# Skip weights loaded as a row, and the first half of the output projection's first block placed between the steps of the last sample stream

## The chip, the cores and the metric

The kernel runs on one core of a Trainium2 chip. TensorE (PE) multiplies, VectorE (DVE), ScalarE (ACT) and GpSimd (POOL) do the elementwise work, and SyncE (SP) issues nearly all transfers. The metric is the time of one execution on the device in microseconds, as the median of several runs.

## The reference

One inference step of a hybrid encoder of two layers over 512 prompt tokens and 8 samples of 16 tokens each (640 columns in all). Layer 0 mixes tokens by sparse attention, layer 1 by a Mamba-2 scan; an MLP follows each mixer. The two places that matter here are the end of the attention (its output projection) and the skip weights of the scan:

```python
def dsa_mixer(h, past_k, past_v, past_ik, w_in, w_o, rel_bias):
    ...
    out = jnp.swapaxes(out, 0, 1).reshape(b, t, N_HEADS * HEAD_DIM)
    return out @ w_o, k, v, ki

def ssd_mixer(h, conv_state, ssm_state, w_in, conv_w, conv_b, dt_bias, a_log, d_skip, norm_w, w_out):
    ...
    dt = jax.nn.softplus(dt_raw.astype(jnp.float32) + dt_bias.astype(jnp.float32))
    ...
    y, final = ssd_scan(xs, dt, A, Bm, Cm, init, blk)
    y = y + xs * d_skip.astype(jnp.float32).reshape(SSM_GROUPS, HEADS_PER_GROUP)[..., None]
```

`w_o` is 1024 x 1024. `d_skip` (the input `ssm_d`) has one number for each of 32 heads.

## The kernel before

Activations lie transposed in SBUF: 1024 features as 8 chunks of 128 partitions, 640 tokens as columns. A product of 32-bit precision is made of three: each operand is split into a high part (ACT copies it to a rounded type: `WH`, `b1H`) and a low part (DVE subtracts: `WL`, `b1L`), and PE adds up high x high, high x low and low x high. A block is 128 output features: 8 chunks x 3 products x 2 halves of 320 columns = 48 matmuls, each with its own load of weights (`chunk_products`, line 203, called by `multiply`). The two halves go to two neighbouring PSUM banks. The weights have two slots. SP loads a slab (`load_slab`, line 178) when the slab two blocks before has been split, ACT and DVE split it (`split_hi` line 191, `split_lo` line 195) when the block two before has been multiplied, and the result is evicted from PSUM by DVE; at the output projection that is `add_to_x` (line 434), which adds it to the residual.

Blocks have numbers: 17 to 24 (`B_O + d`) are the output projection. The weights of 17 and 18 are split while the queries are projected, long before they are used. `tail_pe` is what PE does from block 17 on.

Ahead of it stand the sample streams, one for each of 8 samples (`sample_stream` on PE, `sample_step` on DVE). In stream b PE turns the probabilities of sample b in two halves (line 2613), turns the heads of sample b - 1 (`turn_sample_heads`, line 2636, from the tile `osm`), weighs the values in two halves (line 2627), and computes the logits of sample b + 1. The last stream has no next sample. DVE normalizes the heads into `osm` (line 3122), PE turns them, ACT and DVE split the turned heads into `b1H` and `b1L` (lines 2843 and 3131). The prompt's heads wait in `hF` as 8 tiles (two groups of 4 chunks x four tiles of 128 tokens, list `TILES`); in step b of the samples one of them is split, by ACT (`heads_hi`, line 2809) and DVE (`heads_lo`, line 3063). DVE counts each low part in the semaphore `otl` ("heads_lo"): 16 when all are there.

Nothing is scheduled automatically: the order on each engine is the order of the code, and the engines meet at semaphores.

`tail_sp` is what SP issues at the same time: the old convolution rows, four slabs of weights for blocks 19 and 20 (8 transfers), then the small weights of layer 1. `dcol` is the skip weights as a column for each pair of heads: partition p of column k holds the weight of head 2k + p // 64. It is loaded by two transfers of 64 partitions x 16 numbers that lie two numbers apart in memory, each number on its own. `dtb` and `negA` are rows of 32 numbers, copied to all partitions. The semaphore `ss_st` counts these four, by 16 each. `dt_dve` (line 881 on) uses `dtb` some 500 us later, in the first group of the scan, and POOL uses `dcol` in line 1053.

Of the kernel before, what the change touches and what calls it, by code (L numbers as in the profile page):

```python
# [23 lines left out]
P = 128  # L24
# [61 lines left out]
def build(nc, A, O, S):  # L86
# [71 lines left out]
    class Block:  # L158


        def __init__(self, c, v=0):
            self.c, self.v = c, v
            self.slot, self.n, self.use = c % 2, c + 2 * v, c // 2 + v
            self.first = isinstance(v, int) and c + 2 * v < 2
            self.out = 6 if c == B_O + 7 else 2 * self.slot

    def settled(eng):

# [39 lines left out]
    def multiply(pe, b, RH, RL, m=P, ready=None, between=None, order=tuple(range(KC))):  # L208
# [12 lines left out]
            last = chunk_products(pe, b, RH, RL, k, n, m)  # L221
        last.then_inc(mm_done, 1)


    def chunk_act(act, nu, i, d, g, H, ready):

# [184 lines left out]
    TILES = [(0, 0), (0, 1), (0, 2), (0, 3), (1, 3), (1, 2), (1, 1), (1, 0)]  # L411
    UNITS = [(a, t, j, gp) for a, t in TILES for j in range(4) for gp in range(2)]
    NU = len(UNITS)
    NPV = NU // 2

    def in_pair(u):
# [34 lines left out]
    conv_old = sc("conv_old", [P, DB * 3, CD // P])  # L451
    conv_new = sc("conv_new", [P, DB * 3 + 3, CD // P])
    dcol = sc("dcol", [P, DI // P])
    dtb = sc("dtb", [P, SH]); negA = sc("negA", [P, SH])
    dt_t = sc("dt_t", [P, NT, SH]); acs_t = sc("acs_t", [P, NT, SH]); ddt = sc("ddt", [P, NT, SH])
    dec = sc("dec", [P, HPG, 4])
    sc("gap", [P, 4, NT])
    TG = T // 4
    ssm_spare = 223584
    gs5 = at("gs5", [P, 4, TG], F32, ssm_spare + 2048)  # L460
    prev = sc("prev", [P, 2, DB, P])
    bc = sc("bc", [P, HPG, T])
# [405 lines left out]
    def dt_dve(dve):  # L868

        v, e, q, p = (dts[:, i] for i in range(4))  # L870
        n = [0]

        def step(ins, wait_last=True):
            ins.then_inc(dts_, 1)
            n[0] += 1
            dve.wait_ge(dts_, n[0])

        t3 = lambda ap: ap.rearrange("p (t h) -> p t h", h=SH)
        dve.wait_ge(dtt, 1)
        dve.wait_ge(rs_step, 11)  # L880
        step(dve.tensor_tensor(t3(v), psum[:, 7, 0:NT * SH].rearrange("p (t h) -> p t h", h=SH),
                               rs5[:, 1].unsqueeze(2).broadcast_to([P, NT, SH]), ALU.mult))
        dve.wait_ge(ss_st, 64)
        step(dve.tensor_tensor(t3(v), t3(v), dtb[:].unsqueeze(1).broadcast_to([P, NT, SH]), ALU.add))
        step(dve.scalar_tensor_tensor(e, v, -1.0, v, ALU.mult, ALU.min))
        dve.wait_ge(dta, 2)
        step(dve.tensor_scalar(q, e, 2.0, None, ALU.add))
        step(dve.reciprocal(q, q))
        step(dve.tensor_tensor(e, e, q, ALU.mult))
        step(dve.tensor_tensor(q, e, e, ALU.mult))  # L890
        step(dve.tensor_scalar(p, q, 1.0 / 15, None, ALU.mult))
        for k in (13, 11, 9, 7, 5, 3):
            step(dve.scalar_tensor_tensor(p, p, 1.0 / k, q, ALU.add, ALU.mult))
        step(dve.scalar_tensor_tensor(p, p, 1.0, e, ALU.add, ALU.mult))
        step(dve.tensor_scalar(v, v, 0.0, None, ALU.max))
        step(dve.scalar_tensor_tensor(dt_t[:].rearrange("p t h -> p (t h)"), p, 2.0, v, ALU.mult, ALU.add))
        dve.scalar_tensor_tensor(t3(p), dt_t[:], -1.0, negA[:].unsqueeze(1).broadcast_to([P, NT, SH]),
                                 ALU.mult, ALU.mult).then_inc(dts_, 1)
# [1024 lines left out]
    def tail_sp(sp):  # L1923
        sp.wait_ge(ttr, NU)
        sp.dma_start(conv_in[:], A["state_conv"][0].rearrange("b r (k c) -> (b r k) c", c=P).rearrange(
            "(q p) c -> p q c", p=P)).then_inc(cv_in, 16)
        for d in range(2, 4):
            load_slab(sp, Block(B_O + d), slab_o(P * d))
        for h in range(2):
            sp.dma_start(dcol[64 * h:64 * h + 64], skew(A["ssm_d"], h, [[0, 64], [2, DI // P]]),  # L1930
                         allow_slow_non_contiguous=True).then_inc(ss_st, 16)
        sp.dma_start(dtb[:], skew(A["ssm_dt_bias"], 0, [[0, P], [1, SH]])).then_inc(ss_st, 16)
        sp.dma_start(negA[:], skew(A["ssm_a_log"], 0, [[0, P], [1, SH]])).then_inc(ss_st, 16)
        for d in range(4, KC):
            load_slab(sp, Block(B_O + d), slab_o(P * d))
        sp.wait_ge(otl, NU // 8 + DB)
        for g in range(32):
            load_pair(sp, g)
        sp.wait_ge(sw_cb, 28)
        load_prev(sp, 0, 0)  # L1940
        load_prev(sp, 0, 1)
        sp.wait_ge(sw_lo, op0(30) + 4)
        load_slab(sp, Block(B_DT), slab(A["ssm_w_in"][0], 0, O_DT + SH - P))
        for j in range(3):
            load_slab(sp, Block(B_SSM + j), ssm_slab(0, j))
        ssm_group_sp(sp, 0, None)
        ssm_group_sp(sp, 1, 0)
        with sp.Fori(2, SG - 1) as g:
            ssm_group_sp(sp, g, g - 1)
        ssm_group_sp(sp, SG - 1, SG - 2)  # L1950

        u = SG - 1
        wo = A["ssm_w_out"][0]
        for m, n in ((tB, SG), (tCB, SG), (c2s, SG), (tX, 2 * SG), (yds, 2 * SG)):
            sp.wait_ge(m, n)
        load_y(sp, 0, 4)
        load_slab(sp, Block(B_OUT + 3), slab(wo, 0, P * 3))
        store_y(sp, u - 1)
        load_slab(sp, Block(B_OUT + 4), slab(wo, 0, P * 4))
        store_states(sp, u, 0)  # L1960
        load_slab(sp, Block(B_OUT + 5), slab(wo, 0, P * 5))
        store_states(sp, u, 1)
        load_slab(sp, Block(B_OUT + 6), slab(wo, 0, P * 6))
        store_prompt_states(sp, u)
        sp.wait_ge(y_st, 16 * (SG - 1))
        sp.wait_ge(y_lo, 8)
        sp.wait_ge(tY, 2 * SG)
        load_y(sp, 8, 4)
        load_y(sp, 12, 2)
        load_slab(sp, Block(B_OUT + 7), slab(wo, 0, P * 7))  # L1970
        for d in range(KC):
            load_slab(sp, Block(B_OUT + 8 + d), slab(wo, D, P * d))
        sp.wait_ge(cnc, 1)
        sp.dma_start(O["conv_sample"].rearrange("l b r (k c) -> (l b r k) c", c=P).rearrange("(q p) c -> p q c", p=P),
                     conv_tok[:, 0:6]).then_inc(store, 16)
        sp.dma_start(O["conv_prompt"].rearrange("l b r (k c) -> (l b r k) c", c=P), conv_tok[0:96, 6]).then_inc(store, 16)
        sp.wait_ge(store, 128)
        for g in range(32, 64):
            load_pair(sp, g)
        for t in range(4):  # L1980
            sp.wait_ge((rs_ready, newton)[t % 2], (8 + 2, 16 + 14)[t % 2] + t // 2)
            sp.dma_start(O["y_prompt"].rearrange("b s d -> (b s) d")[P * t:P * t + P, :], y_tok[:, t]).then_inc(store, 16)

        for s, n in ((pv_st[0], SG), (pv_st[1], SG), (sp_st, SG), (y_st, SG - 1), (store, 8 + NT)):
            sp.wait_ge(s, 16 * n)

    def tail_pool(pool):
        pool.wait_ge(otl, NU // 8 + DB)
        mlp_pool(pool, 0)
        pool.wait_ge(sw_mm, OPS)  # L1990
        pool.memset(raw[:, :, 0:3], 0.0)
        pool.memset(CE[:], 0.0)
        pool.wait_ge(cvo, 1)
        pool.wait_ge(ss_st, 64)
        ssm_group_pool(pool, 0, None)
        ssm_group_pool(pool, 1, 0)
        with pool.Fori(2, SG - 1) as g:
            ssm_group_pool(pool, g, g - 1)
        ssm_group_pool(pool, SG - 1, SG - 2)
        gate_y(pool, SG - 1, 0)  # L2000
        gate_y(pool, SG - 1, 1)
        pool.wait_ge(sp_st, 16 * SG)
        mlp_pool(pool, 1)

    def tail_pe(pe):

        for d in range(KC):
            multiply(pe, Block(B_O + d), b1H, b1L)
            if d == 3:
                pe.wait_ge(cv_in, 16)  # L2010
                for q in range(6):
                    last = pe.transpose(bank(4, 768, 2)[:, q * P:(q + 1) * P], conv_in[:, q], ident)
                last.then_inc(cvt, 1)
# [145 lines left out]
    with nc.Block() as block:  # L2159
# [200 lines left out]
        def _(pe):  # L2360
# [278 lines left out]
            def sample_stream(b, s, i):  # L2639
                last = b_is(b, DB - 1)  # L2640
                turn_probs(b, 0)
                if not g_is_first(b):
                    turn_sample_heads(b - 1)
                if not last:
# [25 lines left out]
                sample_stream(b, b % 2, b // 2)  # L2670
            sample_stream(DB - 2, 0, DB // 2 - 1)
            sample_stream(DB - 1, 1, DB // 2 - 1)
            turn_sample_heads(DB - 1)
            pe.wait_ge(otl, NU // 8 + DB)
            tail_pe(pe)

        @block.scalar
        def _(act):
# [124 lines left out]
                act.activation(OT[:], bank(7), ACT.Copy).then_inc(rbc, 1)  # L2803

            def heads_hi(w):
                a, t = TILES[w]
                act.wait_ge(oe, NU // 8)
                sl = (slice(0, P), slice(4 * a, 4 * a + 4), slice(t * P, (t + 1) * P))
                act.activation(b1H[sl], hF[sl], ACT.Copy).then_inc(oth, 1)
# [58 lines left out]
        def _(dve):  # L2868
# [188 lines left out]
                                  bank(6).rearrange("p (j q) -> p j q", j=4), ALU.mult).then_inc(oe, 1)  # L3057

            def heads_lo(w):
                a, t = TILES[w]  # L3060
                dve.wait_ge(oth, 3 * w + 1)
                sl = (slice(0, P), slice(4 * a, 4 * a + 4), slice(t * P, (t + 1) * P))
                dve.tensor_tensor(b1L[sl], hF[sl], b1H[sl].bitcast(F32), ALU.subtract).then_inc(otl, 1)
# [129 lines left out]
```

## Time and profile before

| | |
|---|---|
| median of 3 runs | 1863.29 us (1863.19 to 1865.09) |
| the profiled execution's own time | 1859.92 us |
| its span | 1858.1 us |
| mean granted clock of TensorE | 0.996 of full speed |
| PE busy | 1828.0 us (98%) |
| DVE, ACT, POOL busy | 1260.9, 799.8, 307.9 us |
| DMA | 178.79 MB, mean 96 GB/s |

The span runs from the first instruction to the last, and all times of rows are counted from its start. A matmul's duration is longer than the distance to the next, since matmuls are pipelined: the distance between starts tells the pace. Idle time stands in brackets behind a row, with what ended it; "issue" there means that the trace shows nothing that the engine waited for.

### The profile page before, as it was taken

Reading aid. Unit: us, or ns where it says so; the run is one execution under the profiler, and the core shown is the slowest. Engines: PE = TensorE matmul, PEld = TensorE weight load, DVE = VectorE, ACT = ScalarE, POOL = GpSimd, SP = SyncE. Lnnn points to the kernel's source line nnn. Section 1 sums busy time; section 2 is a strip of 40 time slices with the busy share of each in tenths; the row PEclk is TensorE's granted clock in tenths of the full one; section 3 lists DMA queues with packets and bytes.
Section 4 is the critical chain, followed back from the end, with each engine's and each line's share of the span. In section 5 each row is a group of like instructions: output and inputs, shape, how many; then the busy total and the mean of one; then the engine's idle time right before and its main releaser. Section 6 shows DMA issues by size and latency. Waiting matters only on the chain.

```text
span 1858.1 us, 35169 instructions
## 1 busy us (share of the span) xinstructions
PE 1828.0 (98%) x13258; PEld 1730.6 (93%) x13258; DVE 1260.9 (68%) x2349; ACT 799.8 (43%) x1412; POOL 307.9 (17%) x343
## 2 busy tenths in 40 slices
PE   8999999899999999999999999999999999999998
PEld 7887667899999999999999999999999999999998
DVE  4498876358677585447878788888535866858553
ACT  4323764344343443335446554566333434334332
POOL 0003553200000000122433434333021000000001
PEclk9999999999999999999999999999999999999999
DMA  6382135232313223223443344434432232322321
GB/s 157 73 131 71 41 103 144 65 96 63 98 52 113 63 74 97 80 58 98 134 137 105 124 123 144 136 104 159 136 90 80 75 97 63 97 79 69 97 64 57
DMA packets 312515, 178.79 MB, mean 96 GB/s; under 512 B 39808, under 2 KB 304960, under 8 KB 311360
## 3 DMA queue, kind: packets, MB, share of 16 engines
q1 hardware_dynamic: 309552, 173.87, 33.1%
q10 hardware_dynamic: 2832, 3.15, 0.5%
q8 instruction: 86, 1.41, 0.3%
q14 instruction: 45, 0.37, 0.1%
HBM read 156.82 MB, written 19.99 MB: 95 GB/s over the span
## 4 chain that ended last, share of the span: by engine, by line
PE 79%; DVE 2%; issue 2%; ACT 2%; DVEq 0%; ACTq 0%
PE psum L1392 28%; PE psum L203 27%; PE psum L1438 15%; PE psum L599 1%; PE psum L2603 1%; PE psum L603 1%; PE psum L563 1%; PE psum L550 1%; PE psum L2627 1%; PE psum L575 1%; ACT HH L1519 0%; PE psum L531 0%; PE psum L627 0%; PE psum L543 0%; PE psum L586 0%
## 5 line engine op out<-in xcount | busy, mean ns | idle before, releaser
L203 PE MATMUL psum<-b2H,WH 128*128 128x320 f32 x912 | 217.0, 319 | 0.6 <-DVE WL L195 0.3
L203 PE MATMUL psum<-b2H,WL 128*128 128x320 f32 x912 | 207.7, 309 | 0.0
L203 PE MATMUL psum<-b2L,WH 128*128 128x320 f32 x912 | 207.5, 309 | 0.0
L191 ACT ACTIVATE WH<-W 128x1024 fp32r<-128x1024 f32 x90 | 95.0, 1055 | 214.5 <-PE psum L203 208.1
L1392 PE MATMUL psum<-b2H,HT 128*128 128x320 f32 x816 | 186.3, 309 | 0.0
L1392 PE MATMUL psum<-b2L,HT 128*128 128x320 f32 x816 | 185.9, 309 | 0.0
L1438 PE MATMUL psum<-HH,HT 128*128 128x320 f32 x544 | 168.6, 310 | 1.2 <-DVE HL L1527 1.2
L1438 PE MATMUL psum<-HL,HT 128*128 128x320 f32 x544 | 168.5, 310 | 0.0
L203 PEld LDWEIGHTS psum<-b2H,WH 128*128 128x128 f32 x912 | 149.0, 188 | 8.4 <-issue 7.0
L1392 PE MATMUL psum<-b2H,LT 128*128 128x320 f32 x672 | 153.1, 309 | 0.0
L203 PEld LDWEIGHTS psum<-b2L,WH 128*128 128x128 f32 x912 | 152.4, 188 | 0.0
L203 PEld LDWEIGHTS psum<-b2H,WL 128*128 128x128 f32 x912 | 152.3, 188 | 0.0
L195 DVE TENSOR_TENSOR WL<-W,WH 128x1024 fp32r<-128x1024 f32 x90 | 130.2, 1447 | 25.0 <-ACT WH L191 24.7
L1466 DVE SCALAR_TENSOR_TENSOR HF<-psum,RS 128x640 f32<-128x640 f32 (+1 forms) x70 | 53.1, 766 | 136.5 <-PE psum L1392 129.2
L245 POOL COPY ACC<-SQ 128x640 f32<-128x640 f32 x4 | 4.3, 1070 | 825.3 <-ACT SQ L232 765.1
L1438 PE MATMUL psum<-HH,LT 128*128 128x320 f32 x448 | 138.8, 310 | 0.0
L1392 PEld LDWEIGHTS psum<-b2L,HT 128*128 128x128 f32 x816 | 136.5, 188 | 0.0
L1392 PEld LDWEIGHTS psum<-b2H,HT 128*128 128x128 f32 x816 | 136.3, 188 | 0.0
L203 PE MATMUL psum<-b1H,WH 128*128 128x320 f32 (+1 forms) x528 | 125.5, 319 | 7.3 <-issue 5.5
L1471 ACT ACTIVATE HF<-HF 128x640 f32<-128x640 f32 (+1 forms) x70 | 48.4, 692 | 189.8 <-DVE HF L1466 189.8
L203 PE MATMUL psum<-b1H,WL 128*128 128x320 f32 (+1 forms) x528 | 121.3, 311 | 0.2 <-DVE WL L195 0.2
L203 PE MATMUL psum<-b1L,WH 128*128 128x320 f32 (+1 forms) x528 | 121.3, 311 | 0.0
(409 smaller groups left out, 4335.3 us busy)
## 6 DMA issues: line engine op xcount, KB each, us to landing
W<-ssm_w_in SPq DMA_DIRECT2D x98, 256.0 KB, 3.1
RW<-mlp_w_up SPq DMA_DIRECT2D x64, 256.0 KB, 3.0
RWx<-mlp_w_up SPq DMA_DIRECT2D x64, 256.0 KB, 3.0
RW<-mlp_w_down SPq DMA_DIRECT2D x64, 256.0 KB, 3.1
RWx<-mlp_w_down SPq DMA_DIRECT2D x64, 256.0 KB, 3.2
bc<-scratch_acs SPq DMA_DIRECT2D x8, 1280.0 KB, 8.0
W<-attn_w_in SPq DMA_DIRECT2D x32, 256.0 KB, 3.9
prev<-state_ssm SPq DMA_DIRECT2D x16, 512.0 KB, 5.4
```

The costliest lines, as they stand in the source:

```text
L191: act.activation(WH[:, b.slot], W[:, b.slot], ACT.Copy).then_inc(w_hi, 1)
L195: dve.tensor_tensor(WL[:, b.slot], W[:, b.slot], WH[:, b.slot].bitcast(F32), ALU.subtract).then_inc(w_lo, 1)
L203: last = pe.matmul(psum[0:m, b.out + h, 0:TH], w[:, b.slot, k, 0:m], r[:, k, h * TH:(h + 1) * TH], start=(n == 0 and i == 0), stop=(n == K ...
L550: last = pe.matmul(bank(4, 1024, 2)[:, 256 * t + P * p:256 * t + P * p + P], Btok[:, t * P:(t + 1) * P], xddt[:, p, t * P:(t + 1) * P], st ...
L563: last = pe.transpose(bank(6, 1024, 2)[:, b * P:(b + 1) * P], prev[:, p, b], ident)
L575: last = pe.matmul(psum[:, 4 + i, 0:256], xddt[r, p, SEQ:T], Bx[r, 2 * i:2 * i + 2].rearrange("p b n -> p (b n)"), start=True, stop=True)
L599: pe.matmul(bank(6, T, 2)[64 * h:64 * h + 64, t * P:(t + 1) * P], xdt[:, p, t * P + 64 * h:t * P + 64 * h + 64], Wm[:, 2 * p + h, t * P:(t ...
L603: pe.matmul(psum[:, 4, (t - 1) * P:t * P], ST[:, t - 1, p * P:(p + 1) * P], C2[:, t * P:(t + 1) * P], start=True, stop=True)
L1392: last = pe.matmul(psum[:, row_bank(g, i // 2) + h, 0:TH], w[:, k], x, start=(kx == 0 and c == 0), stop=(kx == 7 and c == 2))
L1438: last = pe.matmul(down_bank(g, i), w[:, k], x[:, DNB[i], k], start=(k == 0 and c == 0), stop=(k == 3 and c == 2))
L1466: dve.scalar_tensor_tensor(t, src, 0.0, rs, ALU.max, ALU.mult).then_inc(h_rl, 1)
L1471: act.activation(t, t, ACT.Square).then_inc(h_sq, 1)
```

## The change

Three edits. (1) `ssm_d` is loaded as a row of 32 numbers into a new tile `drow`, the same on all 128 partitions, by one transfer; DVE makes `dcol` from it by two strided copies in `dt_dve`. `ss_st` counts three transfers. (2) Block 17 is multiplied in halves (`half_products`), each half in a bank of its own, 6 and 7. The half of columns 0 to 319 is cut in three pieces: 6 matmuls in the last sample stream, 5 behind it, 13 behind the last turning of heads; the other half follows in `tail_pe` after the wait for all heads. (3) The prompt's tiles are split in the order `SPLIT_ORDER`, so that those of tokens 0 to 383 come first.

```diff
@@ class Block
-            self.out = 6 if c == B_O + 7 else 2 * self.slot
+            self.out = 6 if c in (B_O, B_O + 7) else 2 * self.slot
@@
+    def half_products(pe, b, RH, RL, h, lo=0, hi=3 * KC):
+
+        for n in range(lo, hi):
+            k = n // 3
+            w, r = ((WH, RH), (WH, RL), (WL, RH))[n % 3]
+            last = pe.matmul(psum[:, b.out + h, 0:TH], w[:, b.slot, k], r[:, k, h * TH:(h + 1) * TH],
+                             start=(n == 0), stop=(n == 3 * KC - 1))
+        return last
@@
+    SPLIT_ORDER = (0, 1, 2, 5, 6, 7, 3, 4)
@@
+    drow = at("drow", [P, SH], F32, 228992)
...
-    ssm_spare = 223584
+    ssm_spare = 223648
@@ dt_dve
-        dve.wait_ge(ss_st, 64)
+        dve.wait_ge(ss_st, 48)
+        for h in range(2):
+            r = slice(64 * h, 64 * h + 64)
+            dve.tensor_copy(dcol[r], drow[r].rearrange("p (k h) -> p k h", h=2)[:, :, h])
@@ tail_sp
-        for h in range(2):
-            sp.dma_start(dcol[64 * h:64 * h + 64], skew(A["ssm_d"], h, [[0, 64], [2, DI // P]]),
-                         allow_slow_non_contiguous=True).then_inc(ss_st, 16)
+        sp.dma_start(drow[:], skew(A["ssm_d"], 0, [[0, P], [1, SH]])).then_inc(ss_st, 16)
@@ tail_pool
-        pool.wait_ge(ss_st, 64)
+        pool.wait_ge(ss_st, 48)
@@ tail_pe
-        for d in range(KC):
+        half_products(pe, Block(B_O), b1H, b1L, 1).then_inc(mm_done, 1)
+        for d in range(1, KC):
             multiply(pe, Block(B_O + d), b1H, b1L)
@@ sample_stream
                 turn_probs(b, 0)
+                if last:
+                    pe.wait_ge(w_lo, B_O + 1)
+                    pe.wait_ge(out_free, B_O - 1)
+                    pe.wait_ge(otl, 11)
+                    half_products(pe, Block(B_O), b1H, b1L, 0, 0, 6)
                 if not g_is_first(b):
                     turn_sample_heads(b - 1)
@@
             sample_stream(DB - 1, 1, DB // 2 - 1)
+            half_products(pe, Block(B_O), b1H, b1L, 0, 6, 11)
             turn_sample_heads(DB - 1)
+            half_products(pe, Block(B_O), b1H, b1L, 0, 11)
             pe.wait_ge(otl, NU // 8 + DB)
             tail_pe(pe)
@@ heads_hi and heads_lo
-                a, t = TILES[w]
+                a, t = TILES[SPLIT_ORDER[w]]
```

On PE, in the last sample stream, before the change (`PRS` are the probabilities, `VP` and `VN` the values, `osm` the normalized heads; line 2636 stands for the heads of sample 6 and then of sample 7):

```order
L2614 MATMUL psum<-cst,PRS 16x128
L2636 MATMUL psum<-cst,osm 128x128 [waits logits_ready,heads_normalized]
L2636 MATMUL psum<-cst,osm 128x128
L2613 MATMUL psum<-cst,PRS 128x128 [waits second_probs_copied,exp_done]
L2613 MATMUL psum<-cst,PRS 128x128 x3
L2614 MATMUL psum<-cst,PRS 16x128
L2627 MATMUL psum<-VP,PTs 64x64 [waits probs_copied,heads_normalized,cached_v_landed1]
```

and after, where the same turnings have the lines 2626, 2627 and 2649:

```order
L2627 MATMUL psum<-cst,PRS 16x128
L230 MATMUL psum<-b1H,WH 128x320 [waits heads_lo,out_free,w_lo]
L230 MATMUL psum<-b1L,WH 128x320
L230 MATMUL psum<-b1H,WL 128x320
L230 MATMUL psum<-b1H,WH 128x320
L230 MATMUL psum<-b1L,WH 128x320
L230 MATMUL psum<-b1H,WL 128x320
L2649 MATMUL psum<-cst,osm 128x128 [waits logits_ready,heads_normalized]
L2649 MATMUL psum<-cst,osm 128x128
L2626 MATMUL psum<-cst,PRS 128x128 [waits second_probs_copied,exp_done]
```

Six matmuls of block 17 stand between the first turning of probabilities and the heads of sample 6, with the three waits in front of the first.

On PE at the seam between the last weighing and block 17, before:

```order
L2627 MATMUL psum<-VN,PTs 64x64 x2
L2636 MATMUL psum<-cst,osm 128x128 [waits logits_ready,heads_normalized]
L2636 MATMUL psum<-cst,osm 128x128
L203 MATMUL psum<-b1H,WH 128x320 [waits out_free,w_lo,heads_lo]
L203 MATMUL psum<-b1H,WH 128x320
```

and after:

```order
L2640 MATMUL psum<-VN,PTs 64x64 x2
L230 MATMUL psum<-b1H,WH 128x320
L230 MATMUL psum<-b1L,WH 128x320
L230 MATMUL psum<-b1H,WL 128x320
L230 MATMUL psum<-b1H,WH 128x320
L230 MATMUL psum<-b1L,WH 128x320
L2649 MATMUL psum<-cst,osm 128x128 [waits logits_ready,heads_normalized]
L2649 MATMUL psum<-cst,osm 128x128
L230 MATMUL psum<-b1H,WL 128x320
L230 MATMUL psum<-b1H,WH 128x320
L230 MATMUL psum<-b1L,WH 128x320
L230 MATMUL psum<-b1H,WL 128x320
```

Five matmuls moved ahead of the last heads, thirteen (four shown) stand behind them, and the wait for all heads now comes only after these.

## Rows read from the trace of the kernel before

**Rows 1.** Part 1 of the page: busy time, share of the span, instructions.
```profile
PE 1828.0 (98%) x13258; PEld 1730.6 (93%) x13258; DVE 1260.9 (68%) x2349; ACT 799.8 (43%) x1412; POOL 307.9 (17%) x343
```

**Rows 2.** Waits of PE: line, releaser, total us, times, longest us.
```profile
PE psum L203 <- issue: 5.5, 1, 5.5
```

**Rows 3.** Timeline of PE: start, us, line, operation [idle before].
```profile
308.89 0.27 PE L2614 MATMUL psum<-cst,PRS 128*16 128x128 f32 x1
309.70 0.41 PE L2636 MATMUL psum<-cst,osm 128*128 128x128 f32 x2 [0.54 <-DVE nmx L3103]
310.47 0.66 PE L2613 MATMUL psum<-cst,PRS 128*128 128x128 f32 x4 [0.36 <-ACT PRS L2830]
...
312.58 0.29 PE L2627 MATMUL psum<-VN,PTs 128*64 128x64 f32 x4
313.62 0.44 PE L2636 MATMUL psum<-cst,osm 128*128 128x128 f32 x2 [0.75 <-DVE osm L3122]
315.04 0.90 PE L203 MATMUL psum<-b1H,WH 128*128 128x320 f32 x2 [0.99 <-DVE b1L L3131]
...
318.35 0.45 PE L203 MATMUL psum<-b1H,WH 128*128 128x320 f32 x2
...
325.96 0.46 PE L203 MATMUL psum<-b1H,WL 128*128 128x320 f32 x2
331.96 0.90 PE L203 MATMUL psum<-b1H,WH 128*128 128x320 f32 x2 [5.54 <-issue]
```

**Rows 4.** Timeline of DVE, the same columns.
```profile
301.62 0.69 DVE L3063 TENSOR_TENSOR b1L<-hF,b1H 128x512 fp32r<-128x512 f32 x1
...
310.07 0.27 DVE L3110 COPY PTs<-psum 16x128 f32<-16x128 f32 x1
...
314.40 0.59 DVE L3131 TENSOR_TENSOR b1L<-psum,b1H 64x128 fp32r<-64x128 f32 x2
...
323.82 0.82 DVE L434 TENSOR_TENSOR xT<-psum,xT 128x640 f32<-128x640 f32 x1 [8.83 <-PE psum L203]
...
338.17 0.82 DVE L434 TENSOR_TENSOR xT<-psum,xT 128x640 f32<-128x640 f32 x1 [11.18 <-PE psum L203]
...
345.21 0.82 DVE L434 TENSOR_TENSOR xT<-psum,xT 128x640 f32<-128x640 f32 x1 [3.87 <-PE psum L203]
```

**Rows 5.** Windows: length, busy of PE, PEld, DVE, ACT, POOL, PEclk, DMA share, GB/s.
```profile
301.00:308.40 7.40, 7.31 (x72) 5.07 (x73) 5.88 (x16) 4.62 (x12) 3.36 (x5) 1.00 0.84 209
313.00:315.00 2.00, 0.44 (x2) 0.20 (x2) 1.82 (x5) 0.54 (x2) 0.00 (x0) 0.96 0.06 5
316.00:318.00 2.00, 2.00 (x9) 2.00 (x9) 0.00 (x0) 0.00 (x0) 0.00 (x0) 0.50 0.05 0
```

**Rows 6.** DMA, 311 to 329 us: packets and sizes; queue: packets, MB, share.
```profile
DMA packets 1936, 0.02 MB, mean 1 GB/s; under 512 B 1935, under 2 KB 1935, under 8 KB 1935
...
q14 instruction: 1, 0.01, 0.1%
```

**Rows 7.** DMA, 329 to 330.5 us.
```profile
q8 instruction: 1, 0.02, 3.9%
```

**Rows 8.** DMA issues (count, KB each, us to landing), then SP's timeline.
```profile
dcol<-ssm_d SPq DMA_DIRECT2D x2, 4.0 KB, 16.6
dtb<-ssm_dt_bias SPq DMA_DIRECT2D x1, 16.0 KB, 20.7
...
309.81 3.11 SPq L1932 DMA_DIRECT2D dtb<-ssm_dt_bias  x1
312.96 6.56 SPq L1933 DMA_DIRECT2D negA<-ssm_a_log  x1
```

**Rows 9.** Window of line 1438 alone: PE, PEld, PEclk, DMA share, GB/s.
```profile
460.00:464.00 4.00, 4.00 (x30) 4.00 (x28) 1.00 0.30 82
```

**Rows 10.** Timeline of DVE and PE in the scan's first group.
```profile
840.78 0.32 DVE L897 SCALAR_TENSOR_TENSOR dts<-dt_t,negA 128x160 f32<-128x160 f32 x1
...
842.31 0.41 PE L685 MATMUL psum<-cst,dts 128*32 128x128 f32 x2
```

More of the change, by code:

```diff
@@ L3059, in heads_lo @@
             def heads_lo(w):
-                a, t = TILES[w]
+                a, t = TILES[SPLIT_ORDER[w]]
                 dve.wait_ge(oth, 3 * w + 1)
```

## The prediction

> **What bounds the kernel now.** I read the page first: PE is busy 1828.0 of 1858.1 us, 98% [rows 1]. So a change pays if it takes time out of PE's own queue, and only by what PE stood still or ran slowly. The view of waits of PE is next. Its whole idle time is some 30 us, and one entry stands out in it: 5.5 us at line 203, once, released by nothing that the trace knows ("issue") [rows 2]. The third view is the timeline of PE around that place [rows 3]. The output projection's first block (block 17) begins at 315.04, after a wait of 0.99 us for the last sample's low halves. Its first twelve matmuls take from 315.04 to 318.35; from then on two take 0.293 us. Block 18 follows at 323.8, runs until 326.4, stands still for 5.54 us in its middle, where the code has no wait, and then begins slowly again, two matmuls in 0.90 us at 331.96. The starts of the DVE additions mark the ends of the blocks: 323.82, 338.17, 345.21 [rows 4]. Block 19 therefore took 7.04 us (48 matmuls of 0.1467 us), block 18 took 14.35 us, and block 17 took 8.78 us.
>
> The slow matmuls are the clock. The granted clock is 1.00 (2.4 GHz) from 301 to 308.4, where PE is busy 7.31 of 7.40 us; PE is busy only 0.44 us between 313 and 315, where the mean of 0.96 puts the fall shortly before 315, and from 316 to 318 the clock is 0.50 (1.2 GHz) [rows 5].
>
> The stop at 326.4 is what needs a reason. Between 311 and 329 us the core's DMA queues move 1936 packets and 0.02 MB, nearly all of under 512 bytes [rows 6]. The two loads of `dcol` consist of 2 x 64 x 16 = 2048 single numbers, were issued at 308.4 and take 16.6 us on average to land; `dtb`, rows of 128 bytes issued right behind them, takes 20.7 us [rows 8]. The page's instruction queue q8 has no packet in that stretch; its next, of 16 KB, falls between 329 and 330.5 [rows 7], and PE starts again at 331.96. I read it so: PE ran out of instructions, because the packet that holds them waited behind the single numbers of `dcol`, some 19 us long (2048 at 1935 per 18 us).
>
> **The change part by part.** (1) `dcol` as a row. 2048 packets become 128, as in the `dtb` load beside it. The instruction packet then comes when it is asked for, PE does not stop in block 18, and its clock does not fall there. Block 18 costs 7.04 instead of 14.35: 7.31 us less. No other wait stands under this one: weights 18 were split long before, and the load for block 21, which SP issues after the split at 326.2, is needed two blocks later.
>
> The Trainium skill has a rule that speaks against this reading. "DMA: Bandwidth & Descriptors", section "Queues, rings and completion order", says that a DMA engine takes turns between its queue rows after each packet, of at most 64 descriptors; an instruction fetch would then pass `dcol` after a few descriptors, and the stop would have another cause. That one packet of another instruction queue, q14, does get through between 311 and 329 [rows 6] is in its favour; the q8 that stays empty until the small packets run out is against it. By this rule term (1) is 0 and the sum is term (2) alone; it is the third rival below.
>
> (2) Block 17 in halves. The same 48 matmuls are issued, each with its own weight load as before, but 24 of them (columns 0 to 319, all prompt tokens) need only the tiles that the reordered head splits finish by sample step 5. The third such wait, on 11 low halves, was met when DVE's split of step 5 ended at 302.3 [rows 4], 6.8 us before PE asks; the waits on weights and banks have been met since the query blocks. Six matmuls go in at about 309.0, behind the transposes of the last first-half probabilities (last one 308.89). At 0.1465 each they end issuing at 309.9, while the transposes of heads 6 stood at 309.70: those slip by 0.2 us. The next step, at 310.47, waits for ACT's exponential anyway [rows 3], so the slip ends there; ACT takes those heads only after its exponential too, so at most 0.1 us goes on. Five go in after the last weighing, whose final group starts at 312.58: from about 312.8 to 313.5. The head transposes wait for DVE until 313.62, so these cost nothing. The last 13 follow the transposes, 313.88 + 13 x 0.1465 = 315.78. The low halves of the last sample are ready at 314.99 [rows 4], so that wait is gone; what is late next is PE's own work, by 0.8 us. The second half takes 24 x 0.1465 = 3.52 us, to 319.30, and the addition starts at about 319.4 instead of 323.82: 4.4 us less. Of these 1.7 are the clock (8.78 us for the 48 matmuls against 7.04), if it stays up; 2.7 are matmuls laid in holes. I take it to stay up, since PE's longest hole from 308.9 to 319 shrinks from 1.1 us with a 0.8 us hole just before it to 0.4 us, and with holes of that size the clock was 1.00 until 313 [rows 3, 5].
>
> Two details of (2). The 24 matmuls of a half now add into one bank in a row, where the blocks alternated between two. The down projection does the same, one bank for twelve matmuls of this shape, and has 28 of their weight loads in 4 us (27 without the one cut at the edge), one each 0.143 to 0.148 us [rows 9]: no cost, and at worst 0.01 us each, 0.3. If instead the 11 inner matmuls hold the last sample's chain for all that they last, the cost is 1.6 us; the rows above say 0.1.
>
> (3) Two copies on DVE, 64 x 16, ahead of the `dtb` addition, and one less wait value on POOL. The shape isn't in the trace. From above, a copy of 16 x 128 took 0.27 us [rows 4]: two and their wait are under 0.6 us; from below, 0. I take 0.4. DVE's decay exponents end at 841.10 and PE uses them at 842.31 without a wait [rows 10]: 1.2 us of cover, so it costs nothing. Without cover it costs 0.4. The new addresses of the tiles cost nothing.
>
> Sum: -7.3 - 4.4 + 0 = -11.7 us. The profiled execution took 1859.92 us (span 1858.1 and 1.8 around it), and would take 1848.2. The median of the runs shown is 1863.29, 3.4 above that execution, and I take the same distance after: 1863.3 - 11.7 = 1851.6 us. Where the timed runs lose their 3.4 us isn't shown. If it is in this same stop, which depends on when packets meet, it goes too: 1848.2.
>
> **Rivals.**
> *The clock falls all the same.* PE still has holes for ACT and DVE between 310 and 313.6. If the clock is at 0.50 for as long as in block 17 now, 1.7 us come back: 1853.3. For it: the clock's fall before 315 came after a stretch that the change only thins. Against: holes of this size before 311 left it at 1.00.
> *The stop stays where it is in time.* If what delays the instruction packet is tied to the moment, not to `dcol`, then PE reaches the same instruction 4.4 us earlier and waits 4.4 us longer: 1863.3, no change. For it: a wait without releaser proves no cause. Against: packets of under 512 bytes fill exactly that stretch.
> *The packet turns up a fixed time after it is asked for*, whatever `dcol` does. Then PE still stops for 5.5 us in block 18 and only term (2) counts: 1858.9. For it: the packet on q14. Against: q8 empty until the small packets run out. The Trainium skill's rule on turns, above, is the page that gives this case.
> *Slower: the row loads are the slow ones.* `dtb` and `negA`, of the form that `dcol` takes now, hold SP for 3.1 and 6.6 us while they are issued [rows 8]. If a row load by itself keeps the queue for 6.6 us, and `dcol` for little, a third one pushes the instruction packet back by 6.6, and PE's earlier arrival (4.4) is lost in the longer stop: 1863.3 + 6.6 = 1869.9. It decides for slower as soon as a row load keeps the queue longer than the two loads of `dcol` do. Against: 1936 packets in 0.02 MB are about 10 bytes each, not 128; rows aren't what fills the stretch [rows 6].
> *The change doesn't do what it says*: the half products could be issued and yet wait. The waits in front of them have been met, as worked out above, so this is small.
>
> **Chances.** Forecast 0.76; clock falls 0.08; fixed time of asking 0.05; no change 0.05; slower 0.03; the rest, 0.03, spread. 0.2%, about what a measurement of this kernel can tell from no change, is 3.7 us, so faster means under 1859.6: the first three cases and most of the rest, 0.90; same 0.06; slower 0.04. The forecast's own range is 1848.2 to 1853.0 (the 3.4 us above; 0.1 + 0.3 + 0.4 and half of the clock's 1.7 at the other end, rounded up to 1.4); with the case of the clock it is 1847.5 to 1855.5, which leaves the cases at 1858.9 and beyond outside.
>
> **What would show it.** Right: the list of PE's waits has no "issue" entry of 5 us; `drow` lands in a few us, and q8 has a packet near 311; the additions of blocks 17, 18 and 19 start near 319.4, 326.4 and 333.5; the clock stays 1.00 through 320; the head transposes of the last sample still start at 313.6. Wrong: a stop without releaser anywhere in blocks 17 to 19 (term 1), a start of those transposes after 314 (term 2), slow matmuls behind 315 (the clock), or a wait of PE at 842 (term 3).

## The result and the profile after

The changed kernel took 1850.56 us in the median of 4 runs (1848.97 to 1852.84), the kernel before 1863.24 (1860.65 to 1865.09): a ratio of 0.9947 with a 95% interval of 0.9926 to 0.9968, 12.7 us less. Forecast were 1851.6 and 11.7 less. The profiled execution took 1848.97 us with a span of 1847.2, 10.9 less than before.

Part 1 of the page after, and an entry of PE's waits, which answer to [rows 1] and [rows 2] (line, releaser, total us, times, longest):

```profile
PE 1824.7 (99%) x13258; PEld 1728.3 (94%) x13258; DVE 1261.5 (68%) x2351; ACT 799.8 (43%) x1412; POOL 307.9 (17%) x343
```

```profile
PE psum L2386 <- DMA x_stage<-x_sample: 1.0, 1, 1.0
```

The entry of 5.5 us without a releaser is gone. A wait of 1.0 us for the first loads of `x_stage` is new; it lies in the first microseconds, where the change does nothing, and it puts all that follows 0.6 us later than it would be. The timeline of PE after, around the place of [rows 3]:

```profile
309.48 0.27 PE L2627 MATMUL psum<-cst,PRS 128*16 128x128 f32 x1
309.50 0.39 PE L230 MATMUL psum<-b1H,WH 128*128 128x320 f32 x1
...
310.46 0.38 PE L2649 MATMUL psum<-cst,osm 128*128 128x128 f32 x2
311.06 0.66 PE L2626 MATMUL psum<-cst,PRS 128*128 128x128 f32 x4 [0.21 <-ACT PRS L2850]
...
313.38 0.41 PE L230 MATMUL psum<-b1H,WH 128*128 128x320 f32 x1
...
314.22 0.43 PE L2649 MATMUL psum<-cst,osm 128*128 128x128 f32 x2
314.40 0.39 PE L230 MATMUL psum<-b1H,WL 128*128 128x320 f32 x1
...
319.91 0.46 PE L203 MATMUL psum<-b1H,WH 128*128 128x320 f32 x2
```

From 309 to 345 the trace lists no wait of PE of more than 0.21 us. Within each piece the matmuls of block 17 start 0.147 us apart, but for the first one behind other work (0.23 to 0.26). The timeline of DVE has the ends of the blocks, as [rows 4] before:

```profile
314.98 0.59 DVE L3151 TENSOR_TENSOR b1L<-psum,b1H 64x128 fp32r<-64x128 f32 x2
320.11 0.82 DVE L444 TENSOR_TENSOR xT<-psum,xT 128x640 f32<-128x640 f32 x1 [4.54 <-PE psum L230]
...
327.15 0.82 DVE L444 TENSOR_TENSOR xT<-psum,xT 128x640 f32<-128x640 f32 x1 [3.87 <-PE psum L203]
```

Counted from the last sample's low halves, so that the later start drops out, the addition of block 17 comes after 5.13 us instead of 9.42 (323.82 - 314.40), and that of block 18 another 7.04 later instead of 14.35. Together 11.6 us; less the 0.6 of the start this is 11.0, near the 10.9 of the spans. The addition of block 19, at 334.19, is another 7.04 later. The clock, and where the instruction packet lies (columns as in [rows 5] and [rows 7]; the window of the queue is 310.5 to 312):

```profile
313.00:315.00 2.00, 2.00 (x27) 1.84 (x24) 1.29 (x4) 0.41 (x3) 0.00 (x0) 1.00 0.00 0
...
316.00:318.00 2.00, 2.00 (x15) 2.00 (x14) 0.00 (x0) 0.00 (x0) 0.00 (x0) 1.00 0.00 0
```

```profile
q8 instruction: 1, 0.02, 5.1%
```

The row `drow` lands 3.6 us after its issue, `dtb` behind it 4.1 instead of 20.7.

### The profile page after: what moved, and what is told of

The parts are those of the page before. It is cut to its first block, busy times and chain, and to the rows that moved or that the text cites. A ratio compares the mean times of both kernels' runs of the same rounds, so it can differ in the third digit from the quotient of the medians.

```text
span 1847.2 us, 35170 instructions
## 1 busy us (share of the span) xinstructions
PE 1824.7 (99%) x13258; PEld 1728.3 (94%) x13258; DVE 1261.5 (68%) x2351; ACT 799.8 (43%) x1412; POOL 307.9 (17%) x343
## 4 chain that ended last, share of the span: by engine, by line
PE 79%; DVE 2%; ACT 2%; issue 2%; DVEq 0%; ACTq 0%
PE psum L1406 28%; PE psum L203 27%; PE psum L1452 15%; PE psum L610 1%; PE psum L2616 1%; PE psum L614 1%; PE psum L574 1%; PE psum L561 1%; PE psum L2640 1%; PE psum L586 1%; ACT HH L1533 0%; PE psum L638 0%; PE psum L554 0%; PE psum L597 0%; PE psum L542 0%
## 5 line engine op out<-in xcount | busy, mean ns | idle before, releaser
L203 PE MATMUL psum<-b1H,WH 128*128 128x320 f32 (+1 forms) x512 | 120.7, 317 | 0.4 <-DVE b1L L245 0.4
L203 PE MATMUL psum<-b1H,WL 128*128 128x320 f32 (+1 forms) x512 | 117.0, 310 | 0.0
L203 PE MATMUL psum<-b1L,WH 128*128 128x320 f32 (+1 forms) x512 | 116.8, 309 | 0.0
```

What stands on the lines that cost most here:

```text
L203: last = pe.matmul(psum[0:m, b.out + h, 0:TH], w[:, b.slot, k, 0:m], r[:, k, h * TH:(h + 1) * TH], start=(n == 0 and i == 0), stop=(n == K ...
```

## Experiments

Eleven more runs were made, in three groups, each group on a chip of its own, beside the kernel before; two of them, before_again and both_again, are the two kernels unaltered. The table puts together what their traces show around the blocks: A, from the start of the last sample's low halves on DVE to the addition of block 17; B, from there to the addition of block 18; the stop of PE without a releaser in block 18. The times are medians; those of before were measured on the same chip.

| kernel | A | B | stop | this | before | ratio, 95% interval |
|---|---|---|---|---|---|---|
| before, first trace | 9.42 | 14.35 | 5.5 | | | |
| before_again | 9.53 | 7.04 | none | 1858.59 | 1859.32 | 1.0003 (0.9981 to 1.0026) |
| the change | 5.13 | 7.04 | none | 1850.56 | 1863.24 | 0.9947 (0.9926 to 0.9968) |
| both_again | 5.12 | 7.04 | none | 1849.55 | 1854.73 | 0.9974 (0.9961 to 0.9988) |
| row_only | 7.98 | 7.04 | none | 1852.53 | 1861.54 | 0.9961 (0.9945 to 0.9976) |
| halves_only | 5.12 | 14.75 | 6.1 | 1851.94 | 1861.54 | 0.9951 (0.9935 to 0.9967) |
| halves_late | 6.75 | 7.04 | none | 1853.40 | 1861.54 | 0.9951 (0.9937 to 0.9965) |
| half_dose | 5.11 | 11.52 | 2.7 | 1852.06 | 1861.54 | 0.9942 (0.9928 to 0.9957) |
| late_numbers | 7.99 | 7.04 | none | 1852.90 | 1854.73 | 0.9990 (0.9978 to 1.0002) |
| halves_late_numbers | 5.11 | 7.04 | none | 1852.12 | 1854.73 | 0.9985 (0.9972 to 0.9998) |
| double_dose | 7.99 | 14.81 | 6.2 | 1867.74 | 1854.73 | 1.0069 (1.0043 to 1.0095) |
| split_double | 7.98 | 8.27 | 1.0 | 1866.98 | 1859.32 | 1.0051 (1.0034 to 1.0069) |
| two_more | 4.82 | 7.05 | none | 1850.90 | 1859.32 | 0.9955 (0.9939 to 0.9972) |

**One part at a time.** row_only is the kernel before with the edits of `drow`, `dcol` and `ss_st` alone.

> Only the skip weights come as a row; block 17 is multiplied as before. Theory (the instruction packet waits behind the 2048 single numbers): the stop of 5.5 us in block 18 and the slow clock after it are gone, block 18 takes 7.04 us, block 17 still takes 8.8 us with a slow start: 7.3 us less than before, 1856. Rival (the stop has another cause): 1863, and the stop is still in block 18.

No stop, B 7.04, as expected; the medians are 9.0 apart, more than 7.3. A part of the rest is in A: 7.98 and not 9.42, though block 17 is untouched and a slow start was expected. The clock did not fall here. Two windows of row_only, with PE just as idle as in [rows 5]:

```profile
313.00:315.00 2.00, 0.52 (x6) 0.20 (x2) 1.65 (x5) 0.54 (x2) 0.00 (x0) 1.00 0.10 19
316.00:318.00 2.00, 2.00 (x16) 2.00 (x15) 0.00 (x0) 0.00 (x0) 0.00 (x0) 1.00 0.00 0
```

halves_only is the changed kernel with the old loads of `dcol` and no copies:

```diff
-        sp.dma_start(drow[:], skew(A["ssm_d"], 0, [[0, P], [1, SH]])).then_inc(ss_st, 16)
+        for h in range(2):
+            sp.dma_start(dcol[64 * h:64 * h + 64], skew(A["ssm_d"], h, [[0, 64], [2, DI // P]]),
```

> Only block 17 in halves and the new order of the head splits; dcol is still loaded as single numbers. Theory: the instruction packet comes when the numbers have drained, at 329 to 330 us, whatever PE does, so PE gets to the end of its instructions some 4.4 us earlier, stops for about 10 us instead of 5.5, and nothing is won: 1863, within 1 us. Rival (the packet comes a fixed time after it is asked for): the stop stays 5.5 us and the gain of 4.4 us is kept: 1858.8.

The theory failed. In the trace the gain of A is kept, the stop is 6.1 us and not 10, and the profiled execution took 1857.8, near the rival's 1858.8. Nor did the packet wait until the numbers had drained. The queues from 327 to 329 us:

```profile
q1 hardware_dynamic: 208, 0.00, 4.7%
q8 instruction: 1, 0.02, 2.9%
```

The packet went through at 327.8, some 16 us after the numbers had begun, and the numbers ran on until about 331. But the median is 1851.94, and the nine runs reach from 1848.3 to 1861.9. Seven of nine lie below 1855, where the changed kernel lies without any stop. So, by these times, the stop was not there in every execution, which none of the theories had.

**The inner matmuls.** halves_late has `half_products(..., 0)` as one piece behind `turn_sample_heads(DB - 1)`.

> The changed kernel with all 24 matmuls of the first half behind the last heads, none inside the last stream. Theory: 11 matmuls of 0.147 us are no longer hidden, 1.6 us more than the changed kernel: 1852.2; the clock stays at 1.00. Rival: with the holes open again the clock falls near 315 and the first matmuls are slow, 1.7 us more: 1853.9. Rival: the inner matmuls held up the last sample, and taking them out costs less than 1 us.

A is 6.75 instead of 5.12, so the 11 inner matmuls are worth 1.63 us, as in the theory. The clock stayed at 1.00 with the holes in front of the last heads open (0.53, 0.36 and 0.75 us, much as in [rows 3]); the one of 0.99 us behind them is filled here too. The median is 1853.40.

two_more puts two more ahead:

```diff
                     turn_sample_heads(b - 1)
+                if last:
+                    half_products(pe, Block(B_O), b1H, b1L, 0, 6, 8)
...
-            half_products(pe, Block(B_O), b1H, b1L, 0, 6, 11)
+            half_products(pe, Block(B_O), b1H, b1L, 0, 8, 13)
```

> The changed kernel with two more matmuls of the first half ahead, in the hole behind the heads of sample 6 (8 behind them in all, then 5, then 11). Theory: they fit into the hole before the second probabilities, so block 17 ends 0.3 us earlier: 0.3 us less than the changed kernel, too little for the timed runs to show, seen in the trace as 8.6 instead of 8.9 us between the low halves of sample 6 and the addition of block 17. Rival: they push the second probabilities back and nothing is won, or up to 0.3 us lost.

The theory held: A is 4.82, 0.30 less, and from the low halves of sample 6 to the addition are 8.61 us instead of 8.92. The median, 1850.90, can't tell it from the changed kernel. By the trace it is the best of all versions, by 0.3 us.

**Is it a race?** halves_only asked for it. both_again is the changed kernel, unaltered.

> The changed kernel once more, to have more runs of it beside those of the kernel before on one chip, and a second trace. Expected: 11 to 12 us less than before; no stop in blocks 17 to 19; the instruction packet before 315.

The trace was as expected, but the medians were only 5.2 us apart: the kernel before took 1854.73 us on this chip, in 29 runs from 1851.0 to 1860.4. So the kernel before was traced once more, unchanged:

> The kernel before, unchanged, for a second trace of it. In another run it took 1854.7 us beside 1849.6 of the changed kernel, where 1861 to 1863 were measured elsewhere. Theory (it is a race: the stop comes only where the single numbers get ahead of the request for instructions): its times fall into two groups some 7 us apart, and a trace with a time near 1854 has the packet before 311 and no stop, one near 1861 has it near 329 and the stop. Rival (the stop is always there and the difference is the clock elsewhere): a trace near 1854 still has the stop.

This execution took 1854.86 us. The additions of its first two blocks, and the instruction queue from 311 to 312 us:

```profile
326.11 0.82 DVE L434 TENSOR_TENSOR xT<-psum,xT 128x640 f32<-128x640 f32 x1 [8.93 <-PE psum L203]
...
333.15 0.82 DVE L434 TENSOR_TENSOR xT<-psum,xT 128x640 f32<-128x640 f32 x1 [3.87 <-PE psum L203]
```

```profile
q8 instruction: 1, 0.02, 8.0%
```

The same kernel, the same 2048 numbers (its second load of them lands after 20.7 us here too), and no stop: the packet went through at 311.15, while the weights of block 20 still moved and some 0.5 us before the numbers began. Whether PE stops in block 18 is decided anew in each execution, by which comes first. What speaks for it is this pair of traces and the spread of the runs; the trace doesn't show the request itself.

The other traces of the same PE code bear it out. Counted from the start of the last sample's low halves, the packet came 5.4 us ahead in before_again and 5.8 ahead in late_numbers (below), both with no numbers in the queue yet; in row_only it came 1.3 ahead, with rows in the queue. In before the numbers began 4.0 us ahead, inside this spread, and the packet came 15.0 us behind. Over all traces: none of the five traces without single numbers has the stop, nor has either trace with the numbers issued late; of the six with the numbers in their old place five have it, and the packet is ahead of the numbers only in the sixth. In all five PE starts again 2.2 to 2.6 us after the packet, though the packet came anywhere from 8.0 to 15.0 us behind the low halves.

Two clean groups, as expected, are not there: the 29 runs of before on the chip of before_again are spread from 1851.7 to 1864.7, and the clock adds steps of its own: in both_again, which has no single numbers, the eight runs with a mean clock of 0.998 or 0.999 took 1847.9 to 1850.5 us and the four at 0.996 or 0.997 took 1851.8 to 1853.2. In this trace it fell before block 17, whose additions come at A = 9.53.

**Which wait is it?** late_numbers adds `sp.wait_ge(otl, NU // 8 + DB)` before the loads of `dcol` of the kernel before, and halves_late_numbers does the same in halves_only.

> The kernel before, whose two loads of single numbers are issued only when all heads are split (about 315 instead of 308.4). They still are 2048 numbers and take about 20 us. Theory (they stop PE only because the instruction packet asked for at 311 to 313 stands behind them): that packet comes at once, the next isn't needed before 343, no stop, 7.3 us less than before. Rival (while the numbers run, PE is slowed or stopped whatever the order): a stop of some 5 us in blocks 18 or 19, no gain.

> Block 17 in halves, and the single numbers as in late_numbers; no row, no copies on DVE. Theory: as the changed kernel within 0.5 us, about 11.6 us less than before, since numbers behind the request cost nothing and the copies cost nothing. Rival: the copies or the row cost or bring something, and it differs from the changed kernel by more than 1 us.

Neither has a stop in block 18 or 19, so numbers behind this packet cause no stop, and the rival of late_numbers is out. They do hold back the packet after it, to 22.7 us behind the low halves where it came 7.7 behind them in row_only, but PE doesn't need that one yet. The 7.3 us of late_numbers did not come: it was 1.8 us below a kernel before that by its times mostly ran without the stop on this chip, and the interval includes no difference. halves_late_numbers was 2.6 us above both_again, not within 0.5. The copies and the row, which its rival had, are not what the trace shows: the weights of block 21 stand behind the numbers in SP's queue. PE in halves_late_numbers where they are first used:

```profile
347.05 0.56 PE L203 MATMUL psum<-b1H,WH 128*128 128x320 f32 x2 [1.19 <-DVE WL L195]
```

The addition of block 20 comes 9.51 us after that of block 19 there (7.47 in late_numbers), a part of which the next blocks make good, since DVE splits the late weights before that addition. From the addition of block 19 to that of block 22 it is 23.23 us, against 21.78 in both_again: 1.4 us lost. In late_numbers it is 21.77, so nothing is lost there. The expectation had weighed the packet against the numbers, but not what a later place of the numbers would do to the slabs behind them.

**How long does the packet wait?** half_dose is the changed kernel with one of the two old loads after the row, its destination `dcol[0:64]`; double_dose is the kernel before with both loads again into a spare tile behind them; split_double is double_dose in loads of 32 partitions:

```diff
-        for h in range(2):
-            sp.dma_start(dcol[64 * h:64 * h + 64], skew(A["ssm_d"], h, [[0, 64], [2, DI // P]]),
+        for h in range(4):
+            sp.dma_start(dcol[32 * h:32 * h + 32], skew(A["ssm_d"], h // 2, [[0, 32], [2, DI // P]]),
```

> The changed kernel, and behind the row one of the two loads of single numbers (1024 of them), used for dcol's upper partitions. Theory: the numbers drain in half the time, 9.6 us, and hold back an instruction packet to about 320 us instead of 310.6; PE needs it at about 322, so there is no stop or one of under 1 us: 1850.6 to 1851.6. Rival (any load of single numbers stops PE for some time, whatever its length): a stop of 2.7 us or more, half of the 5.5, and a slow clock behind it.

> The kernel before with the two loads of single numbers issued twice, the second time into a spare tile (4096 numbers, 38 us). Theory (the packet waits until the numbers have drained): it comes near 348, the stop in block 18 grows from 5.5 to about 24 us, 18 us slower than before. Rival (it takes its turn after a fixed time or share, about 18 us): the stop stays at 5.5 us and the time within 1 us of before. A packet after 64 numbers of each DMA engine's share would come near 320 and there would be no stop.

> As double_dose (4096 single numbers), in eight loads of 32 partitions instead of four of 64. In double_dose the packet came at 329.9, 20 us after the first numbers and 19 us before the last. Theory (the packet waits for two loads of its DMA engine's share, 64 numbers and 9.6 us each): with shares of 32 numbers it comes after about 10 us, near 320, and there is no stop in block 18. Rival (it waits some 19 us whatever the loads' size): 329, and the stop of 5 to 6 us. The wait for the weights behind the numbers, near 356, stays in both.

double_dose says the same as halves_only against my theory. Its queues, a line each from 311 to 329 us, from 329.8 to 331, and from 331 to 349:

```profile
q1 hardware_dynamic: 1934, 0.01, 4.7%
...
q8 instruction: 1, 0.02, 4.9%
...
DMA packets 1947, 0.02 MB, mean 1 GB/s; under 512 B 1937, under 2 KB 1947, under 8 KB 1947
```

The packet comes at about 330 while the small packets run on at the same rate to 349. It does not wait until they have drained; it passes them some 19 us after the first. The stop is 6.2 us and not 24, as the rival had it. What does wait for all of them is the next load in SP's own queue, the weights of block 21, and this is where the kernel loses:

```profile
332.25 0.90 PE L203 MATMUL psum<-b1H,WH 128*128 128x320 f32 x2 [6.17 <-issue]
356.45 0.90 PE L203 MATMUL psum<-b1H,WH 128*128 128x320 f32 x2 [3.33 <-DVE WL L195]
```

The time of 1867.74, 13.0 above before, lay between the two expectations (18 and 0), by a mechanism that was in neither. It is also measured against a kernel before that mostly ran without the stop on this chip. In split_double the packet came between 324 and 325, the stop was 1.0 us:

```profile
326.56 0.56 PE L203 MATMUL psum<-b1H,WH 128*128 128x320 f32 x2 [0.97 <-issue]
```

That is 14 us after the first numbers: not the 10 us that two shares would give, nor the 19 of its rival. Whether the size of the loads sets the wait isn't shown. Loads of 64 partitions gave 19 us in two traces but 16 in halves_only, and no trace shows when the packet was asked for. The kernel loses 7.7 us all the same, since PE waits 7.9 us for the weights of block 21 behind the numbers. In half_dose the packet came at 327.3, some 12 us after the numbers began and about when they ended, with a stop of 2.7 us and a slow clock behind it, as the rival had it; a stop of under 1 was expected. Its median of 1852.06 and its fastest runs of 1848.7 suggest that this too happened in part of the runs only.

## Why the prediction was right, and where it was not

*The stop (term 1).* Right in place, cause and size for the executions that have it: B went from 14.35 to 7.04, 7.31 as worked out, row_only removes it alone, double_dose and halves_only keep it, and PE starts again 2.2 to 2.6 us after the packet in all five traces with a stop. Not seen was that it is not always there. One trace and three runs of nearly the same time looked like a fixed cost; in the 29 runs of the third measurement the kernel before was 7 to 8.5 us faster than in the first two. The forecast met the first measurement because, by their times of 1860.65 us and more, its four executions of before had the stop; that was luck. Against the medians beside both_again it would have been 6.5 us too much.

*From the trace to the median.* Luck had a part here too. The two profiled executions are 10.9 us apart, not 11.7, most of the missing 0.8 being the later start. The median of before lies 3.4 us above its profiled execution, and I took the same distance after; it was 1.6, which brought the 10.9 up to 12.7. The upper end of the range was also mis-added: 0.1 + 0.3 + 0.4 and half of 1.7 make 1.65, not 1.4.

*Why the packet waits.* The step "the packet waited behind the single numbers, some 19 us long" is right in that the numbers hold it back and wrong in the picture of a drained queue. The Trainium skill's rule that I set against it ("DMA: Bandwidth & Descriptors", "Queues, rings and completion order": turns between queues, a packet of at most 64 descriptors at a time) fits double_dose and halves_only better, where the packet passes between the numbers. I had dismissed its turn as short, "after a few descriptors". The numbers go at 1935 in 18 us, in 16 shares if the load is spread evenly, which is one in 0.15 us for a share: 64 of them last 9.6 us, and two such turns the 19 that were seen in before and double_dose. That is an estimate. With the 9 to 17 descriptors that the same section of the Trainium skill calls typical of a packet, a turn would be 1.4 to 2.6 us by the same estimate, and no trace has so short a wait. split_double's 14 us doesn't fit two turns of 4.8, nor halves_only's 16 two of 9.6, so what sets the length of the wait is open.

*The halves (term 2).* 4.29 us between the two traces against 4.4. Its parts were 2.7 of overlap, measured as 7.98 - 5.12 = 2.86, and 1.7 of clock, measured as 9.42 - 7.98 = 1.44. The prediction set the 8.78 us from the first matmul of block 17 to its addition against the 7.04 from one addition to the next; at full clock that stretch is 0.3 us longer, which it counted as clock. Of the overlap 1.63 are the inner matmuls (halves_late), the other 1.2 are the 13 that stand in front of the wait for the last low halves. The overlap is there in every trace. The clock is not: of six traces of block 17 unsplit it fell in two (before and before_again) and stayed at 1.00 in four, with the same holes. In none of the seven with the halves did it fall there, not even in halves_late with most of its holes. Two of six against none of seven is too little to show that the halves keep the clock up. So 1.4 to 1.6 us is what it costs when it falls, and nothing that the traces show tells when. The heads of sample 6 are turned 0.18 us later, as worked out, and nothing of it goes on: the last sample's low halves come 3.79 us after those of sample 6, before and after.

*The signs.* The additions of blocks 17 to 19 came at 320.11, 327.15 and 334.19, the packet at 310.6. The last head transposes started at 314.22, past the 314 named as a sign of being wrong; less the 0.6 us of the later start they stand where they stood (313.62), and the additions are 0.1 to 0.2 us behind the times forecast.

*The copies (term 3).* They take 0.17 us each, DVE's exponents end at 830.47 and PE uses them at 831.29 without a wait: 0.8 of the 1.2 us of cover is left, and 0.4 was the estimate.

*The rivals.* "Slower, the row loads are the slow ones" fell at once: `drow` lands in 3.6 us. "A fixed time after it is asked for", whatever `dcol` does, fell with row_only. "The stop stays where it is in time" fell with halves_only: where its profiled execution has the stop, it keeps the gain of the halves, and the packet came 16 us after the first numbers where it was 19 in before.

Something stays open: why halves_only, with the numbers in place, seldom has the stop. Six more matmuls of PE, each with its weight load, before the last heads of sample 6 may shift who is first; no trace shows the request, and it wasn't tried apart. The order may be set earlier: in before, row_only, halves_only and half_dose the instruction packet before this one came 13.2 to 13.4 us ahead of the last low halves, in the nine other traces 14.9 to 15.1, and SP's loads stand 0.75 us nearer to the low halves too. The three of these four that have numbers have the stop; but so have double_dose and split_double of the nine.

## What to carry over

Loads of single numbers keep the DMA share at 0.05 and still hold up what comes behind them: loads in the same queue waited for all of them, and PE's instruction packet, unless it was ahead, came 12 to 19 us after the first number. A stop of an engine with no releaser in the middle of straight code is worth a look at the instruction queue in the DMA view; and one trace of such a stop is one draw, so trace the kernel twice before pricing it. Matmuls that depend on part of their input can be put into the holes of the stage before, priced by the distance between starts.

## What the runs showed of the hardware that was not expected

- 4096 numbers of 4 bytes kept the queue busy from 310 to 349 us at a DMA share of 0.05, which looks like an idle queue.
- The same kernel has or lacks a stop of 5.5 us by which comes first, an instruction packet or a load of single numbers: in before_again the packet was 0.5 us ahead (before and before_again). By the times, the share of executions with the stop differed between chips or measurements: medians of 1863.2, 1861.5, 1854.7 and 1859.3 for one kernel.
- The granted clock, at equal holes of PE (0.44 us busy in the same 2.0 us, from 1.4 us ahead of the last low halves, in all six traces of block 17 unsplit), fell in two traces and stayed at 1.00 in four.
